# The even mixer of a four-layer decoder kernel: logarithms in two groups, decays among the projections, u ahead of z, state update ahead of the head norm

## The reference, cut to what matters

```python
hn = rms_norm(h, ln_mix_e[i])
proj = hn @ w_in_e[i]
a_uv, b_qkv, b_z, b_beta, b_a = jnp.split(proj, split_at, axis=-1)
a_out = gmlp_spatial_gate(jax.nn.gelu(a_uv), gmlp_v_gain[i], gmlp_ws[i], gmlp_bs[i])
b_out = gated_deltanet(b_qkv, b_z, b_beta, b_a, ...)
h = h + jnp.concatenate([a_out, b_out], axis=-1) @ w_out_e[i]
```

## Time and profile before

| | us |
|---|---|
| median of 3 runs | 2200.59 (2199.46 to 2202.91) |
| profiled execution, its own time | 2200.82 |
| its span, first to last instruction | 2199.0 |
| PE busy in the span | 2052.9 |
| DVE busy | 1083.2 |
| ACT busy | 916.8 |
| POOL busy | 172.2 |

### The profile page before, as it was taken

How to read it: one execution, slowest core, us unless ns; L and a number is a source line. 1 busy time by engine, 2 the same in 40 slices (tenths; PEclk the granted TensorE clock), 3 DMA queues, 4 the chain that set the end, 5 groups by cost and what they waited for, 6 DMA issues and landing times. The chain is left out here.

```text
span 2199.0 us, 27461 instructions
## 1 busy us (share of the span) xinstructions
PE 2052.9 (93%) x11261; PEld 1637.0 (74%) x11261; DVE 1083.2 (49%) x1732; ACT 916.8 (42%) x1673; POOL 172.2 (8%) x134
## 2 busy tenths in 40 slices
PE   6988988999999989999999999988999799989888
PEld 5667877888888777656888888777887677856567
DVE  4456535434333552565543443545346546355763
ACT  5464224323223553575432332454343522245562
POOL 1010000000000000342000000000000100023440
PEclk9999989999999999999999999998999899999999
DMA  4211102333332222111333332213321231210001
GB/s 135 77 58 39 40 20 87 96 98 99 97 104 82 92 70 91 63 39 48 97 96 96 96 96 96 77 59 92 97 85 39 76 115 59 95 39 20 20 1 67
DMA packets 117682, 162.38 MB, mean 74 GB/s; under 512 B 6074, under 2 KB 80070, under 8 KB 117558
## 3 DMA queue, kind: packets, MB, share of 16 engines
q1 hardware_dynamic: 114502, 150.47, 21.5%
q0 software_dynamic: 2768, 9.10, 1.4%
q10 hardware_dynamic: 288, 1.05, 0.1%
HBM read 158.52 MB, written 2.10 MB: 73 GB/s over the span
## 5 line engine op out<-in xcount | busy, mean ns | idle before, releaser
L437 DVE TENSOR_TENSOR WL<-RAW,WH 128x1024 fp32r<-128x1024 f32 (+1 forms) x283 | 346.1, 1225 | 409.9 <-ACT WH L507 409.5
L507 ACT CAST WH<-RAW 128x1024 fp32r<-128x1024 f32 (+1 forms) x283 | 293.3, 1038 | 417.4 <-PE PSUM L541 417.3
L541 PE MATMUL PSUM<-XH,WH 128*128 128x512 f32 (+4 forms) x1128 | 427.3, 379 | 10.5 <-DVE AR L445 5.0
L541 PE MATMUL PSUM<-XL,WH 128*128 128x512 f32 (+4 forms) x1128 | 414.1, 367 | 0.0
L541 PE MATMUL PSUM<-XH,WL 128*128 128x512 f32 (+4 forms) x1128 | 414.0, 367 | 0.0
L541 PE MATMUL PSUM<-WH,HP 128*128 128x512 f32 x1024 | 317.8, 390 | 1.9 <-DVE WL L437 1.9
L541 PE MATMUL PSUM<-WH,XH 128*128 128x512 f32 (+1 forms) x608 | 244.0, 401 | 22.2 <-DVE WL L437 7.9
L541 PEld LDWEIGHTS PSUM<-XH,WH 128*128 128x128 f32 (+3 forms) x1128 | 212.6, 188 | 53.0 <-issue 8.9
L541 PEld LDWEIGHTS PSUM<-XL,WH 128*128 128x128 f32 (+3 forms) x1128 | 212.5, 188 | 39.6 <-issue 5.8
L541 PEld LDWEIGHTS PSUM<-XH,WL 128*128 128x128 f32 (+3 forms) x1128 | 212.0, 188 | 35.4
L541 PE MATMUL PSUM<-WL,XH 128*128 128x512 f32 (+1 forms) x608 | 235.3, 387 | 0.0
(11 more groups left out here) (236 smaller groups left out, 2540.2 us busy)
## 6 DMA issues: line engine op xcount, KB each, us to landing
RAW<-in_w_mlp_dram SPq DMA_DIRECT2D x64, 1024.0 KB, 5.3
RAW<-in_nsa_w_in_dram SPq DMA_DIRECT2D x14, 1024.0 KB, 5.2
RAW<-in_w_in_e_dram SPq DMA_DIRECT2D x12, 1024.0 KB, 5.3
RAW<-in_w_qkv_o_dram SPq DMA_DIRECT2D x12, 1024.0 KB, 5.1
RAW<-in_gla_w_in_dram SPq DMA_DIRECT2D x12, 1024.0 KB, 5.3
RAW<-in_w_ple_gate_dram SPq DMA_DIRECT2D x8, 1024.0 KB, 5.0
RAW<-in_w_out_e_dram SPq DMA_DIRECT2D x4, 1024.0 KB, 5.1
RAW<-in_w_out_o_dram SPq DMA_DIRECT2D x4, 1024.0 KB, 5.2
```

Of the source, the lines that this page charges most:

```text
L437: return x.do.tensor_tensor(o, a, b, op)
L507: a.do.copy(hi, r).then_inc(*up("w_hi", "w_hi", j))
L541: m = p.do.matmul(o, l, r, start=start and i == 0, stop=stop and i == len(pairs) - 1)
```

## The change

- ev takes banks 0 to 3 instead of the next four in turn.
- The logarithms of the l2 norms come in two groups on ACT, all four heads of q at i = 4 and all four of k at i = 9; before, they came two heads at a time at i = 4, 5, 9 and after z(0). The squares of q come at i = 1, those of k at i = 6, four at a time. PE's sums and gates move with them.
- All four decays are made among the projections, each in its own buffer: subtractions at i = 3, Exps at i = 4, strict masks at i = 6 and 7. The strict product goes into AT's place.
- u is projected and loaded ahead of z, in the places that z had, and the pieces between the levels are dealt out anew: three ahead of m0 as before, 15 up to the end of level 4, and none in level 5.
- The q k products are copied out by ACT and multiplied with the decay on POOL.
- m6's copies go from ACT to DVE, and ACT turns to yu at once after each diagonal copy.
- In the chunk loop the eg banks are no longer kept, the product of the old state with q (`carried`) is separate from the new part (`within`), the state's update stands ahead of the head norm, and the head norm is cut in parts that follow one block later.

The diff, cut to its core (some removed lines are left out, the bullets say what they did):

```diff
@@ -21,7 +21,7 @@
...
-G_US, G_LM, G_L0T, G_N = 0, 128, 448, 512
+G_US, G_LM, G_L0T, G_ID, G_N = 0, 128, 448, 512, 576
...
@@ -124,8 +125,8 @@
...
+    F(w, 0, 512)
...
-    F(w, 0, 512)
...
@@ -1011,7 +1013,7 @@
...
-        DT = [XN[:, 0, 0:512], XN[:, 0, 512:1024], XN[:, 1, 0:512], XN[:, 1, 512:1024]]
+        DT = [quad(XN[:, n // 2, 512 * (n % 2):512 * (n % 2) + 512]) for n in range(4)]
...
@@ -1068,7 +1070,7 @@
...
-            toks(p, ("ev",), normed(EVEN), after=after,
+            toks(p, ("ev",), normed(EVEN), after=after, banks=(0, 1, 2, 3),
...
@@ -1077,26 +1079,24 @@
...
-                if i in (3, 4):
-                    pe_l2(p, 0, (2 * i - 6, 2 * i - 5))
-                elif i == 6:
-                    pe_gate(p, 0)
-                elif i == 7:
-                    for g in range(1, 4):
+                if i in (2, 3):
+                    pe_l2(p, 0, (2 * i - 4, 2 * i - 3))
+                elif i in (7, 8):
+                    pe_l2(p, 1, (2 * i - 14, 2 * i - 13))
+                if i in (8, 9):
+                    for g in (2 * i - 16, 2 * i - 15):
...
-                elif i in (8, 9):
-                    pe_l2(p, 1, (2 * i - 16, 2 * i - 15))
-            feat(p, ("ez", 0), EVEN)
+            feat(p, ("eu", 0), EVEN)
...
-            feat(p, ("ez", 1), EVEN)
+            feat(p, ("eu", 1), EVEN)
...
-                for job in [("ez", 2), ("ez", 3)] + [("eu", m) for m in range(4)]:
+                for job in [("eu", 2), ("eu", 3)] + [("ez", m) for m in range(4)]:
...
@@ -1109,14 +1109,14 @@
...
-            beside(1)
+            beside(2)
...
-                beside(1)
...
+                    beside(1)
...
@@ -1125,7 +1125,8 @@
...
-                beside(2 if lv < 5 else 1)
+                if lv <= 4:
+                    beside(3 if lv == 1 else 2)
...
@@ -1138,13 +1139,12 @@
...
+                    ps.take(*job)
...
@@ -1153,7 +1153,6 @@
...
-                            ps.drop(*job)
...
@@ -1169,6 +1168,23 @@
...
+            def carried(n):
+                ps.take("o", n, keep=True)
+                p.wait_ge(*ps.empty("o", n))
+                p.wait_ge(*at("qd"))
+                if n:
+                    for h in range(4):
+                        p.do.matmul(bank("o", n)[:, 128 * h:128 * h + 128], SS[:, h, :], QN[:, h, n, :], start=h == 0,
+                                    stop=False, skip_group_check=True)
...
+            def within(n):
+                p.wait_ge(*at("qk_decayed", n))
+                for h in range(4):
+                    m = p.do.matmul(bank("o", n)[:, 128 * h:128 * h + 128], VN[n % 2][:, h, :], QK[:, n, h, :],
+                                    start=n == 0 and h == 0, stop=True, skip_group_check=True)
+                m.then_inc(*ps.filled("o", n))
...
+            gm_product()
...
@@ -1181,25 +1197,15 @@
...
+                carried(n)
...
+                if n:
+                    head_norm(n - 1)
+                within(n)
...
@@ -1291,80 +1297,85 @@
...
+                if i == 1:
+                    act_squares(a, 0, range(4))
...
+                elif i == 4:
+                    act_l2(a, 0, range(4))
+                    for n in range(4):
+                        act_decays(a, n)
+                    a.wait_ge(*at("v_var"))
+                    step(a, act(a, va, va, ACT.Ln, scale=1.0 / 128, bias=EPSC))
+                    act(a, va, va, ACT.Exp, scale=-0.5).then_inc(*up("v_scale", "v_scale"))
+                elif i == 6:
+                    act_squares(a, 1, range(4))
...
+                    act_l2(a, 1, range(4))
+                    a.wait_ge(*at("gl"))
+                    act(a, slot(0), slot(0), ACT.Exp).then_inc(*up("decayed", "decayed"))
+            gate(0)
+            gate(1)
+            for n in range(4):
+                a.wait_ge(*ps.full("qk", n))
+                a.do.copy(QK[:, n, :, :], quad(bank("qk", n)[:, :])).then_inc(*ps.read("qk", n))
+            gate(2)
...
+            gate(3)
...
+                z_gate(m)
...
+            for g in range(4):
+                a.wait_ge(*at("ut", g))
+                a.wait_ge(*ps.full("ez", 3))
+                a.do.copy(XH[:, g, :], UT[:, g, :]).then_inc(*up("gm_hi", "gm_hi", g))
...
+            def head_square(n):
+                a.wait_ge(*ps.full("o", n))
+                a.wait_ge(*tm_clear("head", n))
+                act(a, tm("head", n), bank("o", n)[:, :], ACT.Square).then_inc(*up("head", "head", n))
...
+            def head_scale(n):
...
+            def head_half(n):
...
+                a.do.copy(XH[:, 4:8, 128 * n:128 * n + 128], quad(tm("head", n))).then_inc(*up("hx_hi", "hx_hi", n))
...
+                    head_square(n - 1)
+                if n > 1:
+                    head_half(n - 2)
+                if n:
+                    head_scale(n - 1)
+                if n == 1:
+                    act_weights(a, first_part["eg", 0] + 4)
+            head_square(3)
...
+            head_half(2)
+            head_scale(3)
+            head_half(3)
...
@@ -1401,41 +1412,35 @@
...
+                m = ts(v, DT[n][:, h, :], GR[:, h, n, :], v4(gc)[:, n, h:h + 1], 0.0, ALU.subtract, ALU.min)
...
+        def dve_strict(v, n):
+            v.wait_ge(*at("c_gdn"))
...
+            tt(v, AT[:, n, :, :], DT[n], b1(UST, 4), ALU.mult).then_inc(*up("decay_strict", "decay_strict", n))
...
+            tt(v, AT[:, n, :, :], quad(bank("at", n)[:, :]), AT[:, n, :, :], ALU.mult).then_inc(*ps.read("at", n))
...
+            for c in HALVES:
...
+            tt(v, y, b1(IDC, 4), y, ALU.subtract).then_inc(*up("y0", "y0", n))
...
+            dve_weights(v, first_part["es",] + 3)
...
@@ -1495,34 +1500,35 @@
...
+                elif i == 3:
+                    for n in range(4):
+                        dve_decays(v, n)
...
+                    dve_l2(v, 0, range(4))
+                elif i in (6, 7):
+                    for n in (2 * i - 12, 2 * i - 11):
+                        dve_strict(v, n)
+                elif i == 9:
...
+                    dve_gate(v, 1)
+            dve_gate(v, 2)
+            dve_gate(v, 3)
+            dve_l2(v, 1, range(4))
...
+            dve_weights(v, first_part["eu", 0] + 3)
...
+            gate(0)
+            dve_weights(v, first_part["eu", 1] + 3)
...
+            gate(1)
+            gate(2)
...
@@ -1537,9 +1543,9 @@
...
-                    dve_weights(v, first_part["ez", 3] + 3)
-                else:
-                    gate(lv - 2)
+                    gate(3)
+                elif lv <= 4:
+                    dve_weights(v, first_part["ez", lv - 2] + 3)
...
@@ -1549,6 +1555,13 @@
...
+                if lv == 4:
+                    dve_weights(v, first_part["ez", 3] + 3)
+            l = HALVES[1]
+            for n in range(4):
+                v.wait_ge(*ps.full("m", 6, n))
+                v.do.tensor_copy(M[l, n, :, :], bank("m", 6, n)[l, 0:256].rearrange("p (h t) -> p h t", h=4)).then_inc(
+                    *ps.read("m", 6, n))
...
@@ -1562,40 +1575,45 @@
...
+            def head_gain(n):
...
+            def head_rest(n):
+                c = slice(128 * n, 128 * n + 128)
...
+                tt(v, XL[:, 4:8, c], quad(tm("head", n)), hi.bitcast(F32), ALU.subtract).then_inc(*up("hx_lo", "hx", n))
...
+            gm_add(*adds.pop(0))
...
+                    v.wait_ge(*ps.full("sn", n))
...
+                if n > 1:
+                    head_rest(n - 2)
+                if n:
+                    head_gain(n - 1)
+            head_rest(2)
+            head_gain(3)
+            head_rest(3)
...
@@ -1622,9 +1640,12 @@
...
-                d = quad(DT[2 * (n % 2)])
...
-                tt(g, d, d, b1(UTR, 4), ALU.mult).then_inc(*up("decay_causal", "decay_causal", n))
+                tt(g, DT[n], DT[n], b1(UTR, 4), ALU.mult).then_inc(*up("decay_causal", "decay_causal", n))
+            for n in range(4):
+                g.wait_ge(*ps.free("qk", n))
+                g.wait_ge(*at("decay_causal", n))
+                tt(g, QK[:, n, :, :], QK[:, n, :, :], DT[n], ALU.mult).then_inc(*up("qk_decayed", "qk_decayed", n))
...
```

More of the change, by code:

```diff
@@ L1140, in gm @@
             def gm(c):
-                for t in range(4):
-                    ps.take("eg", c, t, keep=True)
                 got = [part(p, "T") for _ in range(2)]
@@ L1191, in pe_even @@
                     several(p, ("sn", n), lambda b: heads_of(b, lambda h: KD[:, n, h, :], lambda h: VN[n % 2][:, h, :]))
-                b = ps.take("o", n, keep=True)
-                p.wait_ge(*ps.empty("o", n))
-                p.wait_ge(*at("qd"))
-                for h in range(4):
-                    o = PS[b][:, 128 * h:128 * h + 128]
-                    if n:
-                        p.do.matmul(o, SS[:, h, :], QN[:, h, n, :], start=True, stop=False)
-                    m = p.do.matmul(o, VN[n % 2][:, h, :], QK[:, n, h, :], start=n == 0, stop=True)
-                m.then_inc(*ps.filled("o", n))
-            while products:
                 gm_product()
+                if n:
```

(35 more changed lines are left out.)

66 lines of the change are left out of this document (2 added, 64 removed).

## The result

The changed kernel takes 2184.29 us (median of 4, 2184.06 to 2184.99) against 2200.03 (2198.55 to 2202.91): ratio 0.9927, 95% interval 0.9910 to 0.9945. That is 15.7 us less; the forecast was 22 less, and a range of 2168 to 2191. The profiled execution took 2184.13 us, its span is 2182.3. In the helper functions, a line of the changed kernel has the number of before plus one (L437 is L438, L541 is L542).

What follows compares the result with a forecast made beforehand. PE, busy 93% of the span, was taken as the bound, so time could only come from its idle and half-clock stretches. The parts left 23.8 us less: 2200.8 to 2177, made 2178 by small latencies; range 2168 to 2191.

Steps and rivals of the forecast that it cites:

- a: Start of the mixer, ev on banks 0 to 3: 3.2 us idle on WL, qkv(0,2) starts 8.1 us ahead, at 68.9.
- b: First group of logarithms: PE idles 11.9 us instead of 8.93, until 133.1; 5.6 us ahead.
- c: Second group of logarithms: new idle of 6.7 us on Ln until 157.9; products end near 182.1, 3.8 us ahead.
- d: Products and levels: 5.15 us wait on y0 goes; level 5 starts at 244.0, not 252.1, 12.0 us ahead.
- e: Level 5 to first gMLP product: xy5 1.35 us late, 1.7 us half-clock loss; 17.0 us ahead, at 256.0.
- f: Chunk loop up to the last product: 42.9 us instead of 53.9; 27.9 us ahead at 299.0.
- g: Tail: 4.1 us given back, fourth output tile ends at 314.9; all after it is unchanged and moves as a block.
- half clock lasts longer: Rival: stretches after 42.6, 151.2 and level 5 bring 10 us at half clock each; 2187 to 2188; chance 0.17.
- The rival that went by it: Products: POOL blocks DVE four times 1.29 us, m0(3) waits 2.5 us; 2181; chance 0.12.
- The table loads: Sign: table loads up to 350 us fall from 25 to about 13.
- The pauses between the output tiles: Sign in the tail: PE idles between output tiles; the prediction is wrong if they run without pauses.
- The 1 us that I had allowed for handovers: Small latencies left out of the parts, some 20 handovers of 0.05 us, turning 2177 into 2178.

Runs made afterwards that it cites:

- experiments 3 to 12: Ten runs, each with one or several edits on top of the changed kernel; measured from 2168.52 us to 2197.22 us.
- experiment 3: Changed kernel with the q k products multiplied by the decay on DVE again, without ACT's copies and POOL's products: 2183.35 us.
- experiment 12: Changed kernel with the first matmul of one projection of the first MLP done nine times more, output unchanged: median 2180.13 us, ratio 0.9901.
- experiment 5: Changed kernel with PE's l2 sums of k one projection later, after qkv(2,2) and qkv(2,3): 2177.01 us.
- experiment 6: Changed kernel with u projection 0 ahead of gates 2 and 3 on PE: 2177.48 us.
- experiment 8: Changed kernel with the logarithms and products of q in pairs of heads again, at i = 4 and 5: 2182.89 us.
- Experiment 9: Changed kernel with DVE's adds of the output tiles one behind the other and weight parts ahead of the last mean and square: 2179.28 us.
- Experiment 11: Changed kernel with the first matmul of one projection of the first MLP done three times more, output unchanged: 2179.31 to 2185.71 us, ratio 0.9919.

## Why the prediction was right or wrong

**The sign and the rough size** came out of the chain of waits, as the prediction read it. By its own parts (forecast, then measured in the changed kernel):

| part | forecast | measured |
|---|---|---|
| a: wait on WL, then qkv(0,2) starts | 3.2 at 45.8; 68.9 | 2.40 at 46.31; 69.24 |
| b: wait on a square of k | 11.9 until 133.1 | 11.28 until 133.53 |
| c: wait on Ln for gate 2 | 6.7 until 157.9 | 6.72 until 158.53 |
| c: products end | 182.1 | 183.2 |
| d: no wait on y0; level 5 starts | 244.0 | 245.42 |
| e: xy5 late; first gMLP product | 1.35; 256.0 | 1.20; 257.49 |
| f: from there to the last product's end | 42.9 | 43.2 |
| g: fourth output tile ends | 314.9 | 316.4 |
| g: "all after it ... moves as a block" | 23.8 ahead | 22.1, then 19.1, 16.7 |

**Parts a to f** hold within 1.5 us each. What drifts is small: at the start 0.5 us (the first wait ends at 46.31 for 45.8), and this belongs to the profiled execution, whose first 256-column matmul starts at 16.07 where experiments 3 to 12, with the same start, have 15.28 to 15.82. By the end of c it is 1.1. The wait that I forecast longer than the old one (11.9 for 8.93) and the new one of 6.7 were both there, and experiments 5 and 6 show that each was avoidable.

**Half clock in the mixer.** I took a loss of 1.7 us behind level 5 and none behind 42.6; in the trace the clock is 1.00 in both windows. That it stayed up behind 42.6 is luck: with the same program up to there it fell in four of eleven profiled executions. The rival *half clock lasts longer* named three stretches, and one of them came: around the wait that ends at 158.5 the clock is at half for some 10 us (0.79 over 151 to 175), in part while PE still waits. The 1.7 us were not spent, and part f still took 43.2 for 42.9: its other terms were about 2 us too small together, 0.9 of it in waits (0.77, 1.74 and 1.46 for 3.1 in all). There two errors cancelled.

**POOL beside DVE.** I took 1.6 us of stretching between bounds of 0 and 5.2; it is 2.8, and m0 did not wait. (The prediction's own terms for a block on DVE, 0.69, 0.85 and 0.42, add up to 1.96 and not to its 2.06; experiment 3 has 1.95, from 178.05 to 180.00.) Experiment 3 shows that this edit gains nothing: without it the kernel is 0.9 us faster. The rows agree with the rule of the Trainium skill (experiment 3). The rival that went by it, four times 1.29 and a wait at m0, still did not come, since two of DVE's four blocks came after POOL's last instruction.

**The table loads** up to 350 us fell from 25 to 13, as forecast, and brought no time by themselves: experiment 8 is 1.4 us faster with one group taken apart and two loads more. The first group's load, ACT's timeline of the changed kernel:

```profile
111.66 1.28 ACT L451 ACT_TABLE_LOAD   x1
112.95 0.69 ACT L455 ACTIVATE TM<-PSUM,CB 128x512 f32<-128x512 f32 x1
```

The next activation begins 1.29 us after the load's start, so nothing is to be seen of the drain that the Trainium skill ("ScalarE: Activation LUTs", "What ACT_TABLE_LOAD costs") adds, and the row was the right price.

**The step that failed is the last sentence of part g**, "All after it is unchanged and PE-bound, and moves as a block". It failed twice. First, the work is unchanged, but its queue is not: the adds of the output tiles now wait for head 3 on DVE, pace each other at 1.55 us, and put PE's next weight parts late (3.79 us for 2.37 before, and half clock behind it, where before had none). I had seen the tail's delay in the tiles and had not gone on to what stands behind them on DVE. The pauses between the output tiles, which I had named as a sign, are 0.15 and 0.44 us only. Experiment 9 mends the queue and gains 5.0. Second, the lead shrinks by 3.1 us between 1412 and 1488, behind waits that are the same in both kernels. Experiment 11 shows nearly the same program without that loss. The cause stays open: nothing here shows what decides whether the clock falls, nor why the changed kernel's four runs lie within 0.9 us of each other while experiments 11 and 12 have two times each.

The sum, profiled execution against profiled execution: 23.8 less was worked out and 16.7 measured. Of the 7.1 missing, 1.7 are lost up to the fourth tile (23.8 - 22.1), 3.0 in the tail (22.1 - 19.1: 1.4 by the longer wait, 1.3 by half clock behind it), and 2.4 after the mixer (19.1 - 16.7: 3.1 lost and 0.7 regained). The 1 us that I had allowed for handovers covers more than half of the first.

## What to carry to other kernels

Where an operand's producer is moved in a queue, the wait is the sum of what stands ahead of it there; follow that queue also past the last instruction that the change touches, to the next weight part or add that somebody waits for. When PE waits for something early in its list although other ready work stands behind it, swap the two: two such swaps and one in the tail brought as much again (15.8 us) as the whole change. And times of one program here lay up to 6 us apart, partly by whether the clock fell behind short waits far from the edit. So compare a gain at a place just behind the edit, by the lead in two traces, before explaining the end's time.
